# Strassen-Winograd MLP on one core: weight forms in quarters, two splits and one product moved

## The reference

```
h = rms_norm(x, norm_ffn_pre[i])          # x: 1024 tokens x 1024, float32
f = square(relu(h @ w1)) @ w2             # w1: 1024 x 4096, w2: 4096 x 1024
x = x + rms_norm(f, norm_ffn_post[i])
```

## Time and profile before

| | us |
|---|---|
| median of 3 runs | 2595.53 (2594.45 to 2597.56) |
| the profiled execution, its own time | 2599.4 |
| its span in the trace | 2597.7 |
| PE busy | 2515.3 (97%) |
| DVE busy | 1478.7 (57%) |
| POOL busy | 1095.7 (42%) |
| ACT busy | 1034.8 (40%) |
| 'down' of layer 0, first product to last | about 940 to 1262 |
| 'down' of layer 1 | about 2270 to 2588 |

### The profile page before, as it was taken

One profiled execution on the slowest core, in us unless ns is written; L12 is line 12 of the kernel. 1 busy time (PEld: TensorE's weight loads), 2 busy tenths in 40 slices (PEclk: granted clock), 3 DMA queues, 4 the chain that ended last, 5 costly groups with the idle time before them and its releaser, 6 DMA issues.

```text
span 2597.7 us, 35503 instructions
## 1 busy us (share of the span) xinstructions
PE 2515.3 (97%) x13100; PEld 2137.3 (82%) x13100; DVE 1478.7 (57%) x1941; ACT 1034.8 (40%) x1541; POOL 1095.7 (42%) x712
## 2 busy tenths in 40 slices
PE   7999999997999999999999999999999999999998
PEld 7998888886888877888898878787897888878886
DVE  3215655649655578677711126666356655688775
ACT  5223221225444434334401138887544444433332
POOL 2211211226555556556312224545424555456554
PEclk9999999999999999999999999999999999999999
DMA  5223112123444464444323544444322444564443
GB/s 171 82 96 114 58 57 81 65 90 105 158 151 153 154 217 156 167 161 166 122 93 120 190 150 104 109 117 100 123 95 95 161 154 154 182 221 159 141 156 127
DMA packets 180418, 342.57 MB, mean 132 GB/s; under 512 B 12224, under 2 KB 95168, under 8 KB 178240
## 3 DMA queue, kind: packets, MB, share of 16 engines
q1 hardware_dynamic: 173632, 311.47, 36.7%
q10 hardware_dynamic: 6656, 29.36, 2.8%
HBM read 235.95 MB, written 104.86 MB: 131 GB/s over the span
## 4 chain that ended last, share of the span: by engine, by line
PE 50%; DVE 5%; ACT 3%; issue 3%; DMA 1%; POOL 1%; SPq 0%; DVEq 0%; ACTq 0%
PE psum L1303 17%; PE psum L1235 11%; PE psum L1048 7%; PE psum L1035 7%; PE psum L1394 4%; PE psum L1364 2%; PE psum L1381 2%; DMA a_raw<-a_forms 1%; DVE stick L2427 1%; ACT brk L1872 1%; DVE ra_lo L2248 1%; POOL rw_lo L977 1%; ACT psum L1878 1%; DVE blk_t L2242 1%; DVE acc L2266 0%
## 5 line engine op out<-in xcount | busy, mean ns | idle before, releaser
L1303 PE MATMUL psum<-rw_hi,ra_hi 128*128 128x512 f32 x896 | 352.8, 394 | 16.6 <-DVE acc L2266 9.1
L1303 PE MATMUL psum<-rw_lo,ra_hi 128*128 128x512 f32 x896 | 351.1, 392 | 0.0
L1303 PE MATMUL psum<-rw_hi,ra_lo 128*128 128x512 f32 x896 | 351.0, 392 | 0.0
L977 POOL TENSOR_TENSOR rw_lo<-blk,rw_hi 128x512 fp32r<-128x512 f32 x152 | 231.8, 1554 | 182.5 <-ACT rw_hi L1694 182.5
L866 POOL TENSOR_TENSOR w_lo<-stage,w_hi 128x1024 fp32r<-128x1024 f32 x50 | 119.8, 2418 | 435.6 <-ACT w_hi L1453 434.8
L2248 DVE TENSOR_TENSOR ra_lo<-a_raw,ra_hi 128x512 fp32r<-128x512 f32 x224 | 231.0, 1039 | 26.1 <-ACT ra_hi L1683 26.1
L1683 ACT ACTIVATE ra_hi<-a_raw 128x2048 fp32r<-128x2048 f32 x56 | 107.4, 1918 | 342.0 <-PE psum L1303 236.7
L2427 DVE TENSOR_TENSOR_SCAN stick<-psum,brk 128x128 f32<-128x128 f32 (+7 forms) x128 | 172.5, 1354 | 115.7 <-ACT psum L1878 115.2
L996 POOL TENSOR_TENSOR brk<-brk,stick 128x128 f32<-128x128 f32 (+7 forms) x128 | 153.0, 1206 | 188.2 <-DVE stick L2427 176.3
L1303 PEld LDWEIGHTS psum<-rw_hi,ra_hi 128*128 128x128 f32 x896 | 169.6, 189 | 56.3 <-issue 14.4
L1303 PEld LDWEIGHTS psum<-rw_hi,ra_lo 128*128 128x128 f32 x896 | 169.6, 189 | 35.9
(11 more groups left out here) (280 smaller groups left out, 6583.8 us busy)
## 6 DMA issues: line engine op xcount, KB each, us to landing
a_raw<-a_forms SPq DMA_DIRECT2D x56, 1024.0 KB, 5.5
a_forms<-a_out SPq DMA_DIRECT2D x64, 512.0 KB, 3.1
blk<-mlp_w_in SPq DMA_DIRECT2D x28, 1024.0 KB, 5.4
a_forms<-a_out SPq DMA_DIRECT2D x32, 768.0 KB, 3.3
stage<-a_w_in_in SPq DMA_DIRECT2D x16, 1024.0 KB, 5.4
stage<-mlp_w_in SPq DMA_DIRECT2D x16, 1024.0 KB, 6.1
raw<-mlp_w_in SPq DMA_DIRECT2D x32, 512.0 KB, 5.3
x_res<-xt SPq DMA_DIRECT2D x24, 512.0 KB, 2.7
```

Source lines behind the costliest of these rows:

```text
L977: ins = pool.tensor_tensor(w[1][:, k, :], src[:, k, :], w[0][:, k, :].bitcast(F32), ALU.subtract)
L1303: mm = pe.matmul(psum[:, down_bank(n, tp), :], ring_a[n % 3][sa][:, k, tp * P:(tp + 1) * P], ring_w[n % 3][sw][:, k, :], start=(p in (1, 2 ...
```

## The change

Three edits, all in and around 'down', in both layers:

1. `block_form` makes one quarter (one instruction) per call. In the loop over steps the quarter `tp` stands behind the addition `(n, tp)` and ahead of the split `(n + 2, tp)`; before, all four stood ahead of the step's first addition. The form's semaphore still rises with its last quarter.
2. In DVE's `boundary`, the four splits of the last step stand ahead of `post_norm(b, 2)`; at the end of the kernel two of them stand also ahead of `add(1, 3)`. At the end of layer 0 `add(2, 2)` moves ahead of `post_norm(b, 4)` and of `lo(1)`.
3. In the last 'up' chunk, P6 follows P5 directly, and P4 of chunk 14 comes behind it.

```diff
-            seq += [(c, 1), (c, 2), (c, 5), (c - 1, 4), (c, 6), (c, 3), (c, 7)]
+            seq += [(c, 1), (c, 2), (c, 5), (c, 6), (c - 1, 4), (c, 3), (c, 7)]
...
-            def block_form(layer, v, s):
+            def block_form(layer, v, s, k):
...
-                for k in range(KU):
-                    got = dve.tensor_tensor(ins[0][:, k, :], ins[1][:, k, :], ins[2][:, k, :], ALU.subtract)
-                got.then_inc(t_sum, 1)
+                got = dve.tensor_tensor(ins[0][:, k, :], ins[1][:, k, :], ins[2][:, k, :], ALU.subtract)
+                if k == KU - 1:
+                    got.then_inc(t_sum, 1)
...
                 for n in range(STEPS - 4):
                     v, j = n // 7, n % 7
-                    if j in (0, 1):
-                        block_form(layer, v, 3 + j)
-                    elif j in (5, 6) and v + 1 < UNITS:
-                        block_form(layer, v + 1, j - 4)
                     for tp in range(HALF_T):
                         down_add(layer, n, tp)
+                        if j in (0, 1):
+                            block_form(layer, v, 3 + j, tp)
+                        elif j in (5, 6) and v + 1 < UNITS:
+                            block_form(layer, v + 1, j - 4, tp)
                         if n + 2 < STEPS:
                             down_split(layer, n + 2, tp)
...
                 pre_n(1)
+                if not onward:
+                    split(0)
+                    split(1)
                 add(1, 3)
-                split(0)
-                split(1)
-                post_norm(b, 2)
+                if onward:
+                    split(0)
+                    split(1)
                 split(2)
                 split(3)
+                post_norm(b, 2)
                 add(2, 0)
...
                 pre_n(3)
+                if onward:
+                    add(2, 2)
                 post_norm(b, 4)
                 lo(1)
-                add(2, 2)
+                if not onward:
+                    add(2, 2)
                 post_norm(b, 5)
```

More of the change, by code:

```diff
@@ L2291, in mlp @@
                     if (c, p) == (CH_M - 1, 5):
-                        block_form(layer, 0, 1)
+                        for k in range(KU):
+                            block_form(layer, 0, 1, k)
                     if (c, p) == (CH_M - 1, 6):
@@ L2298, in mlp @@
                             down_split(layer, 1, k)
-                        block_form(layer, 0, 2)
+                        for k in range(KU):
+                            block_form(layer, 0, 2, k)
                 for n in range(STEPS - 4):
                     v, j = n // 7, n % 7
-                    if j in (0, 1):
-                        block_form(layer, v, 3 + j)
-                    elif j in (5, 6) and v + 1 < UNITS:
-                        block_form(layer, v + 1, j - 4)
                     for tp in range(HALF_T):
                         down_add(layer, n, tp)
+                        if j in (0, 1):
+                            block_form(layer, v, 3 + j, tp)
+                        elif j in (5, 6) and v + 1 < UNITS:
+                            block_form(layer, v + 1, j - 4, tp)
                         if n + 2 < STEPS:
```

## The result

The changed kernel takes 2613.8 us (median of 4 runs, 2612.7 to 2614.2). The kernel before, run beside it, takes 2596.6 us (2594.5 to 2598.5). The ratio is **1.0063, 95% interval 1.0051 to 1.0075**: slower by 13.2 to 19.5 us, where 0.4 us faster was forecast. The spans of the two profiled executions are 2611.0 and 2597.7 us; that of before lay above its median, so the traces show 13.3 us of the difference.

The account below looks back on a forecast made before the run. 'down' was taken as bound by TensorE's matmuls, so only PE's idle time could change. Terms +1.9 + 5.5 - 3.5 - 4.3 = -0.4 us gave 2599.0 against the profiled 2599.4, a median of 2595.1; range 2587.5 to 2605.

Parts of the forecast that it names:

- The sum: Layer 0 start +1.9, layer 1 start +5.5, layer 0 end -3.5, kernel end -4.3: together -0.4 us.
- step 4's wait: PE ahead of step 4 of 'down': new idle of 2.4 us in layer 0 and 5.4 in layer 1, both cold.
- the steady state: Units 1 and 2 of 'down': quarters cost nothing, with a cover of 2 us; PE has no bracket.
- the two ends: End of layer 0 -3.5 us (-2 to -4.5); end of the kernel -4.3 us (-3.5 to -4.6).
- the hand-over's wait for POOL: Ahead of (0,0) of 'down': PE starts 1 us later in layer 0, 2.7 us later in layer 1, cold.
- form 4 ends at 972.8: DVE, layer 0: form 4's last quarter ends at 972.8, before at 968.5, so step 4 can start at 991.2.
- 18.4 us from form to step: Chain from form 4's end through load, ACT and POOL to step 4's start: 18.4 us, as before, in both layers.
- rival c: Four loads of one burst end together, 5.0 us later at six places: +22 to +28 us, 2617 to 2623; chance 0.03.
- rival (b): Units 1 and 2, load behind block "11": the 2 us cover is used up, +8 to +14, 2603 to 2609; chance 0.17.
- The work is the same: DVE, forms in quarters: same work, one quarter 0.6 us alone and 1.1 to 1.2 us beside POOL.
- The rule against the trace: Exclusive port lock would put 2.4 us more on POOL's chain ahead of step 4, time 2600; prediction said the trace disagrees.
- Rival (a): Loads are no gate, form 4's late end is hidden: 2578.7 us, or 2587 with half of it; chance 0.17.

Follow-up runs that it names:

- e2: The kernel before with only the reordering at the two ends (splits ahead of the post-norm, add(2,2) earlier): 2593.2 us, ratio 0.998.
- e12: The changed kernel with form 3 whole again ahead of step 0's additions, the other forms in quarters: 2606.7 us, ratio 1.0036.
- e6: The changed kernel with DVE's order in each quarter made form, addition, split instead of addition, form, split: 2615.0 us, ratio 1.0063.
- e1: The kernel before with only the forms in quarters; the ends and the order of 'up' as before: 2613.8 us, ratio 1.0067.
- e3: The kernel before with only P6 moved directly behind P5 in the last 'up' chunk: 2601.8 us, ratio 1.0014.
- e4: The changed kernel with form 4 whole again ahead of step 1's additions, the other forms in quarters: 2598.6 us, ratio 0.9999.
- e11: The changed kernel without the P6 move and with step 4's activations load ahead of the load of block "11": 2592.8 us, ratio 0.9978.
- e5: The changed kernel with step 4's activations load issued ahead of the load of block "11" on SP's queue: 2595.8 us, ratio 0.9988.

## Why the prediction was wrong, point by point

**The step that failed.** It is the time of form 4's end, and with it of step 4. The sum let form 3 in quarters cost nothing, took 1.4 us of a head start off, and put form 4's end at 972.8 and step 4's wait at 2.4 and 5.4 us; the runs show 976.6 and waits of 6.5 and 7.2. Smaller parts of the miss are the load behind form 4 (1.2 us), the steady state, put at nothing (1.06 and 1.54 us), and the two ends (2.6 us too much gain).

**Right: the places.** The prediction named step 4's load behind block "11" as what edit 1 touches, the hand-over's wait for POOL, and the steady state of unit 1 and 2 as the narrowest place. All brackets that it said would go are absent from the changed kernel's trace (two of them from e2's as well), and the large new ones stand where it said. Those in unit 2 don't: there it had said that PE has no bracket, and had named a wait in units 1 and 2 as a sign that it is wrong. The load of block "11" went out 8.05 us later in layer 0 (968.60, then 976.65), not 4 to 6. The sizes of all four terms were too favourable.

**The term "form 4 ends at 972.8" (layer 0).** It ended at 976.6, 3.8 us later. The sum let step 1's additions begin at 963.85 - 1.4 = 962.45 and gave 4.7 + 5.7 = 10.4 us from there to the last quarter. They began at 966.72, and the last quarter ended 9.9 us later. So the block of step 1 was reckoned rightly, even a little dear, and 4.3 us were lost before it, in step 0. Three quarters of form 3, which used to run in DVE's wait for step 2's data, came behind it: 2.8 us. The splits beside them got dearer beside POOL: 0.6 us. And DVE came out of that wait only 0.5 us earlier than before (957.50, before 957.99), not 1.4. e12 agrees: with form 3 whole, step 1's additions began at 963.89, 2.8 us earlier, and the block took 10.4 us. In layer 1 step 1 began late by the same 4.3 us (2306.11, less the 6.1 us by which everything comes later there, makes 2300.0; 2295.65 was reckoned); its block took 9.9 us where 12.3 had been taken, with the form at 6.80, and form 4 ended 1.9 us late.

The price of a quarter was wrong too, but it didn't make the miss: beside POOL an addition, a quarter and a split took 3.4 us, not 2.9 (e6), and with POOL idle 1.8, which made up for it.

**The term "18.4 us from form to step".** 19.7 in layer 0 and 19.6 in layer 1. The load landed (issue to ACT's start) in 9.0 us in both, 7.6 before; four loads went out within 2 us in place of two. In e12 the same load, second in the same burst of four, landed in 7.8 us (issued at 974.76, ACT at 982.56). So the burst alone isn't the reason, and what adds 1.2 us is open. In neither do the loads end together (rival c, 5 us later).

**Their sum.** Layer 0: step 4 started at 996.25, not at 991.2, +5.05; with the forecast's +1.9 and unit 2's 1.06 this makes 8.0 of the measured 8.8, and 0.8 us stays unassigned. Layer 1: less the 6.1 us by which everything comes later there, step 4 started at 2329.5, not at 2326.3, +3.2; with 5.5 and 1.54, 10.2 of 10.4. The bound of the prediction, 1.5 us for the form's end and 0 to 4 for the term, was too narrow: it had tried the length of a quarter from both sides, but not what form 3's quarters do to step 0.

**The steady state, rival (b).** It was half right. The place is right (POOL's low parts for step 4 of unit 2), only in one unit of each layer, 1.06 and 1.54 us. The cause is another: the load behind form 4 took no longer than before, 8.5 us from the form's end at 1133.2 to

```profile
1141.75 1.92 ACT L1683 ACTIVATE ra_hi<-a_raw 128x2048 fp32r<-128x2048 f32 x1 [19.70 <-DMA a_raw<-a_forms]
```

(8.7 before), but the form ended 4.1 us behind the start of the unit's step 2 (1129.1), where 1.3 was reckoned. DVE ran full in the four steps with forms. The window of 43.6 us, four steps, that ends with that start, in the changed kernel, and the one that lies likewise in the kernel before:

```profile
1086.30:1129.90 43.60, 43.60 (x194) 36.11 (x193) 41.75 (x46) 15.14 (x8) 32.19 (x20) 1.00 0.23 74
```
```profile
1077.50:1121.10 43.60, 43.60 (x194) 36.10 (x193) 37.83 (x48) 14.90 (x8) 23.76 (x16) 1.00 0.34 114
```

DVE's busy time, third, is 41.75 of 43.60 in place of 37.83; POOL's, fifth, has risen too, with 20 instructions in this window and 16 in the other. "The work is the same" was the false sentence: the instructions are, their time beside POOL isn't. Over the whole trace DVE's 1941 instructions took 1502.0 us in place of 1478.7, and POOL's 712 took 1115.9 in place of 1095.7.

**The hand-over.** As replayed. POOL's low parts in layer 0 ended at 941.5, 0.7 later than reckoned (the last four took 6.33 us and not 6.0):

```profile
935.20 6.33 POOL L977 TENSOR_TENSOR rw_lo<-early,rw_hi 128x512 fp32r<-128x512 f32 x4
```

In layer 1 (0, 0) moved by 9.4 us, 6.1 of it from ahead: 3.3, where 2.7 was reckoned. Step 4's wait hides it in layer 0 and not in layer 1 (e1); by itself edit 3 costs 3.6 us (e3). The 1.6 us charged to each late start came true here (clock 0.65 and 0.50), but the charge isn't steady: in e3, behind the same 3.11 us of idle in layer 0, the clock stayed at 1.00.

**Edit 2.** Direction right, sizes 1.9 for 3.5 and 3.3 for 4.3, 2.6 us too much. PE's brackets in 'down' went as forecast. In layer 0 PE then waited for DVE ahead of the pre-norm's transposes, 1.20 and 1.98 us in place of 0.86, and in e2 the same: DVE's chain of norms was late next, as said, and gave less. It met a wait that had not been counted,

```profile
1266.42 0.16 DVE L1967 RECIPROCAL rstd<-rt 128x1 f32<-128x1 f32 x1 [2.01 <-ACT rt L1505]
```

that is, ACT's part of the pre-norm. That this wait accounts for the 1.6 us is argued, not shown. At the kernel's end 0.6 of the missing 1.0 us are brackets that stayed (0.18 and 0.46 us). The slow stretches that went with the old brackets aren't in every execution either: behind idle of 2.39 and 2.70 us at the same two places the clock stayed at 1.00 in e1.

**The rule against the trace.** The prediction said that four splits in the time of three POOL instructions disagree with an exclusive lock. That was a misreading: POOL's four ended at 932.09 + 6.01 = 938.10, so only the first 2.8 of the splits' 4.57 us lay beside POOL. Likewise the 4.67 us of form 4 in the kernel before, from which the price of 1.2 us for a quarter beside POOL came: POOL was idle in the middle of it, for 1.11 us up to 966.19. POOL in the kernel before:

```profile
966.19 6.89 POOL L977 TENSOR_TENSOR rw_lo<-blk,rw_hi 128x512 fp32r<-128x512 f32 x4 [1.11 <-ACT rw_hi L1694]
```

Both rows fit two operations at 1.7 us and two at 0.6. Where POOL works throughout, the rows have one DVE operation over two SBUF tiles for each POOL instruction of about 1.7 us, with copies between them (the changed kernel, e6) or without (6.80 for four, 6.87 in e4). The Trainium skill, page "SBUF — State Buffer", section "SBUF: two separate sides", says that of such a DVE operation and a GpSimd operation that reads SBUF, the one that starts first gets the shared ports for its whole instruction and the other blocks. The trace agrees as to the turns; a turn of 1.71 us is somewhat less than POOL's 1.29 alone and DVE's 0.6 alone together. The result lies beyond the 2600 that the rule gave, since it too was reckoned at POOL's chain only, and not at DVE's.

**Rival (a)** fell: the loads are the gate. **Rival (c)** gave 2617 to 2623, near what was measured, for a reason that isn't the case.

## What to carry to other kernels

An instruction group cut in quarters and spread among others starts as early as before but ends much later, and who waits for its end pays: look first for the waiter, and then for what stands behind the waiter in an in-order queue. A load that has no condition belongs ahead of one that waits; here that order alone is worth 4.7 us before the change and 19 us after it. Price a group in its new neighbourhood: an addition, a quarter and a split on DVE took 3.4 us beside a busy POOL and 1.8 without it. And before a duration counts as one "beside" another engine, look whether that engine worked all the while: in two rows here it didn't.

## What was not expected of the hardware

- A DVE subtraction of 128x512 with both operands in SBUF takes 0.68 us alone and 1.18 or 1.78 beside POOL: 1.78 right behind another such operation, 1.18 behind a copy out of PSUM (the changed kernel and e6). The copy out of PSUM stays at 0.68. Four in a row took 2.49 us alone, 6.80 or 6.87 (e4) beside a POOL that worked throughout, and 4.67 where POOL paused for 1.11 us.
- POOL's subtraction of the same size took 1.29 us and 1.71 us beside that pattern (13.68 for eight, in e11 and the changed kernel).
- A load of 1 MB landed in 5.1 or 5.2 us (e5) alone, and behind another one in 7.6, 7.8 (e12) or 9.0 us (the changed kernel).
- TensorE's clock fell to 1.2 GHz behind idle of 1.92 us (e1, 2488.62: 0.64 over the next 3.5 us) and stayed at 2.4 GHz behind idle of 3.11 us (e3, 940.90: 1.00). So what an idle stretch costs beyond itself, 1.6 us or nothing, can't be told from its length here.
